# Logits as four strips, q, k and v of the first head side by side in the front, and each convolution one step later in the engines' order

## What is computed

```python
def hybrid_mixer(h, w_in, ...):                      # h = rmsnorm(x), 512 x 1024
    proj = h @ w_in
    gu, gv, q, k, v, gate, b_logit, a_logit = split_cols(proj, IN_SIZES)   # the logits: 4 + 4 columns
    y_a = chunk_spatial_gating(gu, gv, ...)
    qkv = silu(causal_dwconv(concatenate([q, k, v]), dn_conv))             # 4 taps, each channel by itself
    q, k = l2norm(q), l2norm(k)                      # by head, 128 channels each
    beta = sigmoid(b_logit)
    g = -exp(dn_a_log) * softplus(a_logit + dn_dt_bias)
    o = gated_delta_rule(q, k, v, g, beta)           # a triangular solve by chunk, then a scan over chunks
    o = rmsnorm(o, dn_onorm) * silu(gate)
    return concatenate([y_a, o]) @ w_out

def memory_cross_attention(h, m, w_q, w_k, w_v, w_o):   # m = rmsnorm(mem), 256 x 1024
    ...
```

## Time and profile before

| | before |
|---|---|
| median of 3 runs | 1588.41 us (1588.2 to 1588.52) |
| the profiled execution: its time / its span | 1590.12 us / 1588.4 us |
| TensorE busy | 1565.5 us, 99% |
| VectorE, ScalarE busy | 875.8 us (55%), 598.9 us (38%) |
| one unit's splitting pass, mean | ScalarE 1.03 us (line 1574), VectorE 1.27 us (line 1845) |
| mean granted clock of TensorE | 0.994 of full speed |

### The profile page before, as it was taken

One profiled execution on the slowest core, in us unless ns is written; L12 is line 12 of the kernel. 1 busy time (PEld: TensorE's weight loads), 2 busy tenths in 40 slices (PEclk: granted clock), 3 DMA queues, 4 the chain that ended last, 5 costly groups with the idle time before them and its releaser, 6 DMA issues.

```text
span 1588.4 us, 20664 instructions
## 1 busy us (share of the span) xinstructions
PE 1565.5 (99%) x8304; PEld 1298.4 (82%) x8304; DVE 875.8 (55%) x1319; ACT 598.9 (38%) x890; POOL 98.5 (6%) x88
## 2 busy tenths in 40 slices
PE   8899999999999999999999999999999999999997
PEld 7788889888778888888888877877888888888887
DVE  6667665554454344444565777643554663564465
ACT  5534333443344232232456434443343431332331
POOL 0000110220020000000040000000002000000000
PEclk9999999999999999999999999999999999999999
DMA  7111113342122323222322222222332232232221
GB/s 259 60 61 53 56 55 107 111 144 77 53 80 93 107 93 102 92 98 76 116 93 93 80 93 93 80 80 80 105 108 93 93 103 97 93 98 102 93 77 56
DMA packets 45021, 147.10 MB, mean 93 GB/s; under 512 B 5120, under 2 KB 8320, under 8 KB 44800
## 3 DMA queue, kind: packets, MB, share of 16 engines
q1 hardware_dynamic: 43200, 142.85, 26.8%
q10 hardware_dynamic: 1728, 2.95, 0.5%
HBM read 143.68 MB, written 2.10 MB: 92 GB/s over the span
## 4 chain that ended last, share of the span: by engine, by line
PE 93%; DVE 3%; issue 2%; ACT 2%; DMA 0%; POOLq 0%; POOL 0%; DVEq 0%; SPq 0%; ACTq 0%
PE bank L1290 27%; PE bank L1292 27%; PE bank L1291 27%; PE bank L1211 1%; PE bank L1496 1%; PE bank L1513 1%; PE bank L1402 1%; PE bank L1217 1%; PE bank L1430 1%; DVE temp L1837 1%; PE bank L1255 1%; DVE temp L1830 1%; PE bank L1435 0%; PE bank L1257 0%; PE bank L1256 0%
## 5 line engine op out<-in xcount | busy, mean ns | idle before, releaser
L1290 PE MATMUL bank<-a_hi,w_hi 128*128 128x512 f32 (+1 forms) x1283 | 501.8, 391 | 1.3 <-DVE a_lo L1857 1.3
L1291 PE MATMUL bank<-a_lo,w_hi 128*128 128x512 f32 (+1 forms) x1283 | 493.4, 385 | 0.0
L1292 PE MATMUL bank<-a_hi,w_lo 128*128 128x512 f32 (+1 forms) x1283 | 493.3, 385 | 0.0
L1845 DVE TENSOR_TENSOR w_lo<-w_raw,w_hi 128x1024 fp32r<-128x1024 f32 (+1 forms) x260 | 330.6, 1272 | 186.6 <-ACT w_hi L1574 186.0
L1574 ACT ACTIVATE w_hi<-w_raw 128x1024 fp32r<-128x1024 f32 (+1 forms) x260 | 268.1, 1034 | 207.7 <-PE bank L1292 198.0
L1290 PEld LDWEIGHTS bank<-a_hi,w_hi 128*128 128x128 f32 x1283 | 241.5, 188 | 53.0 <-issue 3.8
L1292 PEld LDWEIGHTS bank<-a_hi,w_lo 128*128 128x128 f32 x1283 | 241.4, 188 | 48.5
L1291 PEld LDWEIGHTS bank<-a_lo,w_hi 128*128 128x128 f32 x1283 | 241.7, 188 | 45.5
L1290 PE MATMUL bank<-b_hi,w_hi 128*128 128x512 f32 (+1 forms) x720 | 276.8, 384 | 0.4 <-ACT b_hi L1709 0.4
L1291 PE MATMUL bank<-b_lo,w_hi 128*128 128x512 f32 (+1 forms) x720 | 275.1, 382 | 0.0
L1292 PE MATMUL bank<-b_hi,w_lo 128*128 128x512 f32 (+1 forms) x720 | 275.1, 382 | 0.0
(11 more groups left out here) (301 smaller groups left out, 1206.3 us busy)
## 6 DMA issues: line engine op xcount, KB each, us to landing
w_raw<-weights_in SPq DMA_DIRECT2D x248, 512.0 KB, 3.3
w_raw<-weights_in SPq DMA_DIRECT2D x8, 384.0 KB, 3.0
x_first<-x_in SPq DMA_DIRECT2D x8, 256.0 KB, 5.6
xs<-x_in ACTq DMA_DIRECT2D x8, 256.0 KB, 4.1
w_raw<-weights_in SPq DMA_DIRECT2D x8, 256.0 KB, 2.5
out<-xs SPq DMA_DIRECT2D x16, 128.0 KB, 1.8
mem_x<-mem_in SPq DMA_DIRECT2D x1, 1024.0 KB, 9.0
w_raw<-front_in SPq DMA_DIRECT2D x5, 192.0 KB, 5.9
```

Of the source, the lines that this page charges most:

```text
L1290: pe.matmul(to, weights_hi[:, at], hi, start=k == k0, stop=False)
L1291: pe.matmul(to, weights_hi[:, at], lo, start=False, stop=False)
L1292: t = pe.matmul(to, weights_lo[:, at], hi, start=False, stop=k == k1 - 1)
L1845: dve.tensor_tensor(lo[:, 0:size], raw[:, n % SLOTS, 0:size], hi[:, 0:size].bitcast(F32), ALU.subtract).then_inc(split_dve.handle, 1)
```

## The change

The logits are no longer a unit. Their weights, 32 columns wide (8 used), come with a load of their own (`logits_in`, 128 KB), VectorE multiplies them by the norm's gain (`front` with n = KT), and TensorE multiplies them with x itself in fp32: k-tiles 0 and 1 into partitions 0 to 31 of one side bank, 2 and 3 into 32 to 63, and so on. The four strips are added up when they are turned, by a matrix with ones at 8 columns in each strip (SUM_STRIPS). With that unit gone, the front's three units are q0, k0, v0, and gate 0 and gate 1 follow; `rates` is cut in two steps, and head 0 is in flight before the filler begins. `conv_qkv` now yields once more ahead of `conv` and not behind it. `q_sums` and `sums` become one step for q or k. All eight memory stages stand behind the first half of gate 3. `mem_v` stands behind the next step of the heads. `root2` becomes `root` with A_TWICE, and two semaphores become one. The diff, cut:

```diff
@@ weight_order
     for h in range(H):
         for part in range(3):
             add("qkv", part * H + h)
-            if h == part == 0:
-                add("logits", 0)
@@ schedule
     def conv_qkv(n):
         yield from halves_and_aside("qkv", n)
-        if n in (0, H):
-            yield
+        yield
         add("conv", n)
         convolved.append(n)
-        yield
...
-        for h in range(H):
-            if h:
-                yield from conv_qkv(h)
-                yield from conv_qkv(H + h)
-            aside.extend([lambda: None] * (2 if h == 0 else 0))
-            aside.extend([lambda h=h: add("q_sums", h), lambda h=h: add("sums", h), lambda h=h: scaled(h)])
+        for h in range(1, H):
+            yield from conv_qkv(h)
+            yield from conv_qkv(H + h)
+            aside.extend([lambda h=h: add("sums", h), lambda h=h: add("sums", H + h), lambda h=h: scaled(h)])
             yield from conv_qkv(2 * H + h)
...
         next(last)
-        for t in range(KT // 2):
+        for t in range(KT):
             add("stage", (A_MEMORY, t))
...
-        for t in range(KT // 2, KT):
-            add("stage", (A_MEMORY, t))
         while aside:
...
             project("xa_wv", n)
+            yield
             if n % VALUE_BLOCKS == VALUE_BLOCKS - 1:
                 add("mem_v", n // VALUE_BLOCKS)
-            yield
...
+    add("front", KT)
+    add("square", (A_INPUT, KT - 1))
+    add("root", A_INPUT)
     for j in range(FRONT):
         add("mm", (j, KT - 1, KT))
+        done.add(j)
+    add("logits")
     first_split(FRONT)
-    add("square", (A_INPUT, KT - 1))
-    query, key, logits, filler = conv_qkv(0), conv_qkv(H), gates(), itertools.chain(projections(), first_memory_keys())
...
+    split_ahead(FRONT)
     add("row", A_INPUT)
...
+    add("logits_leave")
+    add("conv", 0)
+    project("gate", 0, kb=KT // 2)
+    add("rates", 0)
+    project("gate", 0, ka=KT // 2)
+    add("conv", H)
+    add("rates", 1)
+    project("gate", 1, kb=KT // 2)
+    add("shape", 0)
+    add("shape", H)
+    add("gate", 0)
+    add("conv", 2 * H)
+    convolved.append(2 * H)
+    project("gate", 1, ka=KT // 2)
+    add("sums", H)
+    add("decays")
+    first = delta_head(0)
+    next(first)
+    filler = itertools.chain(projections(), first_memory_keys())
+    aside.extend([lambda: scaled(0), lambda: add("gate", 1), lambda: add("sums", 0)])
+    in_flight, waiting = [first], list(range(1, H))
     while waiting or in_flight:
@@ tensor_program
+                elif kind == "logits":
+                    q.wait_ge(*front_dve.at(KT))
+                    for t in range(KT):
+                        q.wait_ge(*x_tile_landed[t].at())
+                    wait_side("logits")
+                    for k in range(KT // STRIPS):
+                        for c in range(STRIPS):
+                            at = c * (KT // STRIPS) + k
+                            t = pe.matmul(side("logits")[strip(c), :], logits_w[:, at, :], x0[:, at, :], start=k == 0, stop=k == KT // STRIPS - 1)
+                    t.then_inc(logits_pe.handle, 1)
...
-                        t = pe.transpose(logits[:, c, :], temp("logits")[0:2 * H, chunk(c)], matrices[0:2 * H, EYE, 0:2 * H])
+                        t = pe.matmul(logits[:, c, :], temp("logits")[:, chunk(c)], half_matrix(SUM_STRIPS)[:, 0:2 * H], start=True, stop=True)
@@ vector_program
+                elif kind == "front" and n == KT:
+                    at = COLUMNS["norm_mix"][0]
+                    q.wait_ge(*front_landed[KT].at())
+                    dve.tensor_tensor(logits_w[:, :, :], logits_w[:, :, :], along(columns[:, at:at + KT], STRIP), ALU.mult).then_inc(front_dve.handle, 1)
...
+                elif kind == "logits_leave":
                     wait_temp("logits")
-                    leave(temp("logits")[0:2 * H, :], "logits", 0).then_inc(logits_dve.handle, 1)
+                    q.wait_ge(*logits_pe.at())
+                    q.wait_ge(*row_act.at(A_INPUT))
+                    dve.tensor_tensor(temp("logits"), side("logits"), rstd[:, :], ALU.mult).then_inc(logits_dve.handle, 1)
@@ sync_program
                     sp.dma_start(raw_front[:, t, :], front_in[t]).then_inc(front_landed[t].handle, 16)
+            sp.dma_start(logits_w[:, :, :], logits_in).then_inc(front_landed[KT].handle, 16)
             load_weights(FRONT)
```

More of the change, by code:

```diff
@@ L42 @@
 FRONT = 3
+STRIP = 32
+STRIPS = P // STRIP
 EARLY = 3
@@ L464, in schedule @@
     project("q2", 0, kb=KT // 2)
-    add("root2")
+    add("root", A_TWICE)
     project("q2", 0, ka=KT // 2)
@@ L647, in temp_turns @@
         return [("-", ("acc", n))]
-    if kind == "logits":
+    if kind == "logits_leave":
         return [("+", ("logits", 0))]
-    if kind == "rates":
+    if kind == "rates" and n == 0:
         return [("-", ("logits", 0))]
@@ L716, in square_turns @@
         return [("+", ("unit", n))]
-    if kind in ("q_sums", "sums"):
-        return [("-", ("unit", n if kind == "q_sums" else H + n))]
+    if kind == "sums":
+        return [("-", ("unit", n))]
     if kind == "out_square":
@@ L727, in side_turns @@
     all_at_once = lambda *names: [("+", name) for name in names] + [("-", name) for name in names]
-    if kind == "root2":
-        return one(("sum2", 0))
     if kind == "root":
@@ L735, in side_turns @@
         return [("+", ("row", n))]
-    if kind == "q_sums":
-        return [("+", ("sums", n))]
+    if kind == "logits":
+        return [("+", ("logits", n))]
+    if kind == "logits_leave":
+        return [("-", ("logits", n))]
     if kind == "sums":
-        return [("-", ("sums", n))]
-    if kind in ("row", "rates", "decays", "mix_bias", "mix", "decay", "turn", "out",
+        return one((kind, n))
+    if kind == "rates":
+        return one((kind, n)) if n == 0 else []
+    if kind in ("row", "decays", "mix_bias", "mix", "decay", "turn", "out",
                 "value_turn", "turn_probs", "attended"):
@@ L1051, in evacuated @@
                 return residual_dve.at(((name, k0), n))
[L1052 removed]
+            first = {"qkv": conv_dve, "gu": spatial_u_dve, "gv": spatial_v_dve, "gate": gate_dve,
                      "xa_wk": mem_k_dve, "xa_wq": query_dve, "ffn_w1": relu_dve, "q2": leave_q_dve,
@@ L1296, in tensor_program @@
                         t.then_inc(half_pe.handle, 1)
+                elif kind == "root" and n == A_TWICE:
+                    q.wait_ge(*square2_pool.at(KT - 1))
+                    wait_side("sum", n)
+                    column_sums(side("sum", n)[:, 0:NC], square_sum2[:, :], root_pe)
                 elif kind == "root":
@@ L1863, in vector_program @@
                     dve.tensor_tensor(total, total, square("square", n)[:, 0:total.shape[1]], ALU.add).then_inc(square_dve.handle, 1)
+                elif kind == "root" and n == A_TWICE:
+                    one, two, both = root_of(A_SECOND)[:, 0:NC], ROOT_TWO[:, 0:NC], ROOT_BOTH[:, 0:NC]
+                    q.wait_ge(*root_pool.at(A_SECOND))
+                    dve.tensor_tensor(both, one, one, ALU.mult).then_inc(root_dve.handle, 1)
+                    q.wait_ge(*root_pe.at(n))
+                    q.wait_ge(*root_dve.at(n, 1))
+                    dve.scalar_tensor_tensor(two, side("sum", n)[:, 0:NC], 1.0 / D, both, ALU.mult, ALU.mult).then_inc(root_dve.handle, 1)
+                    q.wait_ge(*root_dve.at(n, 2))
+                    dve.tensor_scalar(two, two, EPS_2, None, ALU.add).then_inc(root_dve.handle, 1)
                 elif kind == "root":
@@ L1916, in vector_program @@
                 elif kind == "sums":
+                    q_square, k_square, k_inverse, k_norm = norms(n % H)
                     q.wait_ge(*sums_pe.at(n))
-                    dve.tensor_scalar(narrow[:, 7 + n, 0:2 * NC], side("sums", n)[:, 0:2 * NC], EPS, None, ALU.add).then_inc(sums_dve.handle, 1)
+                    dve.tensor_scalar(q_square if n < H else k_square, side("sums", n)[:, 0:NC], EPS, None, ALU.add).then_inc(sums_dve.handle, 1)
                 elif kind == "norms":
```

142 lines of the change are left out of this document (57 added, 85 removed).

## The result

| | before | after |
|---|---|---|
| median of the timed runs | 1588.32 us (1588.2 to 1588.52, 4 runs) | 1578.03 us (1577.46 to 1578.32, 4 runs) |
| ratio to before, 95% interval | | 0.9935 [0.9919, 0.9951] |
| profiled execution: time / span | 1590.12 / 1588.4 us | 1578.32 / 1576.2 us |
| mean granted clock of TensorE | 0.994 | 0.996 |

The change made the kernel 10.3 us faster; 10.5 were forecast (1577.9 us, range 1572.5 to 1584.5). The sum was right, but two of its terms were not, and they happened to cancel. The rest of the text is about that.

The account below looks back on a forecast made before the run. TensorE, busy 99% of the span, was taken as the bound. Start -6.7, later convolutions -0.8, memory stages -1.0, `mem_v` -4.4, clock +2.4 sum to -10.5 us: 1577.9 us, range 1572.5 to 1584.5.

Parts of the forecast that it names:

- Part 1: Logits in four overlapping strips instead of a projection: strips 1.9 us, turn 0.8, TensorE work down 3.0 us.
- one strip at a time: Worst case of the no-overlap rival: logit matmuls run singly, +5.1 us, 1583.0 us; chance 0.12 for that rival alone.
- Part 2, the chain: VectorE and ScalarE steps up to head 0's first `level_y`: 6.7 us gained, new waits of 2.4 and 3.7 us.
- the estimate by the chain: Gain up to `level_y` (0,1) from following its last-ending steps: 7.3 us; adding up terms gave 6.2, and 6.7 was taken.
- Part 2, the clock: TensorE's clock falls at the new 3.7 us wait at `level_y` (0,1), costing 2.4 us.
- rival (a): The clock doesn't fall at the new wait at `level_y` (0,1): 2.4 us better, 1575.5 us; chance 0.17.
- Side banks: New turns of the four side banks might remove or add about 0.7 us; none taken, 2 us kept for the range.
- Part 3: Each q, k, v convolution a step later: two 0.4 us waits of the heads' steps go, -0.8 us.
- The 2 us in hand: Slack before TensorE asks for a `level_x` evacuation queued behind a convolution: 5.8 us against about 8, no new wait.
- rival (d): Convolutions ahead of heads' evacuations make TensorE wait at eight later q, k, v steps, 1.9 us each giving 1593.1; chance 0.15.
- Part 4: Memory stages behind gate 3's first half, -1.0 us; `mem_v` later so squares of heads 2 and 3 go first, -4.4.
- Rival (c): Squares of heads 2 and 3 wait for something else until `xa_wv` 3 ends: 4.4 us stay, 1582.3; chance 0.08 alone.

Follow-up runs that it names:

- e4: The changed kernel with all eight logit matmuls into one strip of 32 output rows, one after the other: 1583.23 us, ratio 0.9962.
- e6: The changed kernel with eleven fp32 matmuls on zeros on TensorE in place of its wait for the squared k0: 1579.04 us, ratio 0.9937.
- e5: The kernel before with only the memory stages all behind gate 3's first half and `mem_v` behind the heads' step: 1582.64 us, ratio 0.9960.
- e9: The changed kernel with each side bank taken by the oldest release instead of in fixed rotation: 1576.56 us, ratio 0.9923.
- e3: The changed kernel with each q, k and v convolution put back directly behind its unit, ahead of the heads' step: 1581.83 us, ratio 0.9954.
- e1: The changed kernel with `mem_v` put back ahead of the heads' step: 1582.22 us, ratio 0.9957.
- e8: The changed kernel with convolutions, memory stages and `mem_v` placed as before, leaving only the strips and the new start: 1587.39 us, ratio 0.9992.
- e12: The kernel before with side banks taken by the oldest release: 1589.58 us, ratio 0.9999.

## Why the prediction was right, step by step

**Part 1: right.** The strips took 1.92 us (1.9 forecast), the turn 0.95, or 0.81 up to the next matmul's start (0.8). e4 makes up the whole difference that was put on one strip at a time, 5.2 us against 5.1.

**Part 2, the chain: right.** The row is copied at 27.8 us, k0 is squared at 41.1, `level_y` (0,1) starts at 61.8; forecast were 29.5, 42.9 and 63.4 with a front that ended 1.9 us later. From the row to the squares it took 13.3 us against 13.4, from there to `level_y` 20.7 against 20.5. The wait for k0 was 2.3 us (2.4 forecast). Against the middle of my two estimates, 6.7 us, 7.0 were measured, nearer to the 7.3 of the estimate by the chain. That one was the better: it follows what ends last, while the sum of terms had to guess at the new waits.

**Part 2, the clock: the step that failed.** I put 2.4 us on the clock's fall at the wait of 3.7 us near 60 us. It fell at the first wait, of 2.3 us, instead; TensorE then came to `level_y` 3.4 us later and waited only 0.5 us there. So the wait of 3 to 4 us near 60 us, which the prediction gave as a sign, didn't come. The prediction names this case itself and prices it at nothing, and e6 bears that price out to within 0.8 us. I had left it out of the sum, as waits of 1.3 and 1.5 us had not moved the clock; the wait of 1.9 in the earlier trace rows, which had, was nearer to 2.4. That one trace was no safe ground either: in e5 the same wait of 1.5 us did bring the clock down (last section). With the first fall in the sum it is -12.9 and the forecast rival (a)'s 1575.5.

**Side banks: the other step that failed.** I took none and kept 2 us for the range. Two new waits of 0.8 us came from the fixed turns, and with the `k_dec` wait of 1.0 the stretch up to `xa_wk` lost 1.5 us where 0.8 were to be gained, 2.3 us off. e9 gets 2.2 of these back. The size was about the 2 us kept; the sign should have been asked for: with four banks in fixed rotation, a new order can meet a bank that is still read, and three times it did.

**Part 3: right in direction, mis-sized.** Moving the convolutions is worth 2 to 3 us in the changed kernel at a like clock (e3; 3.8 by the medians) and not 0.8. The 2 us in hand held: no wait at a later convolution is over 0.5 us, which refutes rival (d).

**Part 4: right**, 5.4 us by the landmarks, 5.5 undone, 5.8 alone. Rival (c) falls with e1.

**The end.** Behind `w_out` the changed kernel lost 0.6 us, 0.4 of it a wait for `b_hi` at L1298 that is in the list above. e1 doesn't have that wait, nor has e5, which keeps the new place of `mem_v`; no experiment was made on it, and its cause stays open.

So the total came out by luck: 2.4 us of clock that did not have to be paid covered 2.3 us of waits that nobody had counted, and the 0.3 us that the chain gained above its forecast made up half of the 0.6 lost at the end. A prediction that hits by its sum is not right by that: the landmarks, compared stretch by stretch, show what the total hides.

## What to carry to other kernels

Follow the chain to the point where it next ends a wait, and price a slower engine by what is left of its delay there: between two waits that another engine's chain sets, 3.4 us lost to TensorE's clock cost 0.8 at most, while 5.4 us off the chain were 5.4 us off the time. Judge a moved step in the order that it will stand in, not by the waits that the old order shows: with the convolutions in their old places and the banks in fixed turns the new start lost most of its 6.7 us again behind `level_y` (0,1) (e8). And where buffers go round in fixed turns, look again at who holds them after every change of order; taking the one that has been free for longest shortened the stretch with these waits by 2.2 to 2.9 us in the changed orders, and by 0.8 in the old one.

## What the runs showed of the hardware

Four fp32 matmuls with 32 output columns each, into four strips of one bank, ran almost wholly beside each other: 8 matmuls of 512 columns in 1.92 us, against 7.05 one after the other.

The length of a single wait did not tell whether TensorE's clock fell behind it. Behind 2.27 us in after, and behind 1.87 us in before, e1 and e8, the granted clock fell to 0.50 or to means between 0.65 and 0.92, the lower level (1.2 GHz) for part or all of a stretch. Behind 1.99 us in e4 and 2.08 us in e3, at 171 us, it stayed at 1.00. And one wait did both: the logits' 1.47 us, with the same program up to there, brought it down in e5, where it ended at 28.9 us, and left it at 1.00 in before, where it ended at 31.2. The wait and the stretches of e5, then the stretches of before, then those of e3:

```profile
PE bank L1323 <- DVE temp L1828: 1.5, 1, 1.5
```

```profile
28.00:32.00 4.00, 3.12 (x12) 2.48 (x13) 1.49 (x6) 1.71 (x5) 0.00 (x0) 0.72 0.93 380
32.00:36.00 4.00, 4.00 (x19) 3.31 (x18) 2.73 (x7) 1.06 (x3) 0.00 (x0) 0.86 0.05 20
```

```profile
28.00:32.00 4.00, 2.53 (x18) 2.15 (x17) 2.92 (x4) 0.72 (x2) 0.98 (x2) 1.00 0.89 306
32.00:36.00 4.00, 3.35 (x17) 2.47 (x16) 1.59 (x8) 2.15 (x6) 0.00 (x0) 1.00 0.44 167
```

```profile
168.00:172.00 4.00, 1.92 (x23) 1.39 (x22) 3.85 (x9) 2.49 (x4) 0.00 (x0) 1.00 0.01 4
172.00:176.00 4.00, 4.00 (x27) 3.54 (x26) 2.59 (x7) 1.97 (x5) 1.28 (x2) 1.00 0.00 0
```

How long it stays low differs as much: behind the same 1.87 us it was low for longer in e8 (0.82, 0.50, 0.83) than in e1 (0.67, 0.90). The runs don't settle what decides. So waits of 1.5 to 2.1 us went either way here, one trace doesn't tell which, and the timings hold some of this chance: those of e3 and e12 part by their mean granted clock, 2 us and more from group to group.

TensorE could leave the front at times that differ by 2.3 us (20.7 to 23.0 us) between executions with the same program up to there, which is as much as several of the terms above; spans are to be compared from that point on.
